# Norm chains at stage borders by half blocks, in a twelve-stage network on one core

## The chip, the core and the metric

One core of a Trainium2 chip runs the whole program. The metric is the device time of one execution in microseconds (us). TensorE (PE) multiplies matrices, VectorE (DVE) and ScalarE (ACT) do the elementwise work, GpSimd (POOL) a little of it, and SyncE (SP) issues the loads. The engines run their own instruction streams in order and wait for each other through semaphores.

## The reference

A sequence of 256 tokens with 1024 features goes through two small models, one behind the other. Every sub-layer reads a normed copy of the residual `h` and adds its product to `h`:

```python
# first model: layer 0 = gated linear recurrence (HGRN), layer 1 = sparse attention (DSA)
hn = rms_norm(h, attn_norm[layer]);  h = h + mixer(hn)
h  = h + conv_ffn(rms_norm(h, ffn_norm[layer]), ...)      # SwiGLU, width 2816, conv of 3 taps
h  = rms_norm(h, final_norm)
# second model: layer 0 = hybrid of attention and conv, layer 1 = gated linear attention (GLA)
h  = h + 0.5 * rms_norm(swiglu(rms_norm(h, g[0]), ffn1), g[1])
h  = h + rms_norm(mixer(rms_norm(h, g[2])), g[3])
h  = h + 0.5 * rms_norm(swiglu(rms_norm(h, g[4]), ffn2), g[5])

def rms_norm(x, gain):                                    # over the 1024 features
    return x * rsqrt(mean(x * x) + 1e-6) * gain
```

So there are six feed-forward stages, ffn 0 to ffn 5, and four mixers, in the order HGRN, ffn 0, DSA, ffn 1, (final norm), ffn 2, hybrid, ffn 3, ffn 4, GLA, ffn 5. Between any two stages stands a chain: product, (norm and gain of the product), add to `h`, norm of `h`, transpose, next product.

## The kernel before, in words

**Products in three parts.** Each float32 operand is split into a high part (fp32r, made by ACT, line 547 for weights and 603 for activations) and a low part (made by DVE, lines 1049, 1108 and 1001, or POOL, line 469). `three` (lines 1561 to 1563) issues high by high, high by low and low by high. The weights come as 1 MB slabs into a ring of four slots (`raw0` to `raw3`).

**Tokens in two blocks.** The 256 tokens are two blocks of 128 (`tb` 0 and 1). A stage's product lies in PSUM as two banks of 512 columns for each block, banks `2*tb` and `2*tb+1`. In an ffn the down projection adds into these banks slab by slab; the last two slabs (`a` and `b_`) run block by block, so that block 0 is complete (`half_done`) while PE still works on block 1.

**The chain of a block at a border**, in the order of the streams, for a stage whose product is normed (after ffn 2 to 5 and after the last two mixers):

- ACT `square_product`: squares of the 1024 columns in PSUM with their sum (L578), then the root (L580);
- DVE `gain_block`: product times gain, two instructions of 512 columns (L1030), after the squares, since both read the banks; reciprocal (L993); `add_normed_block`: one instruction of 1024 columns into `h` (L1035). Without such a norm there is only `add_block` (L1022), 1024 columns;
- ACT `square_h`: squares and sum of `h` (L578), root (L580); DVE reciprocal and `scaled_block` (L1012), two of 512 columns, which gives `xn`;
- PE `turn_block`: 8 transposes of `xn` (L1647); ACT 8 high parts `x_hi` with the gain (L603); DVE 8 low parts `x_lo` (L1001); then the next product, which waits for `x_lo` chunk by chunk (L1561).

PE has other work to put between the blocks. In ffn 0, 1, 3 and 5 block 1 is turned in the middle of the second slab of block 0; in ffn 2 and ffn 4 (`late`) after it; in each case the product of block 1 then needs its `x_lo`. After the 24 matmuls of block 1's first slab PE transposes the first products of block 0 (`turn_tokens`, L1705); these must have been copied out of PSUM by ACT (L614) first. In front of ffn 2, ffn 4, the hybrid and GLA, PE runs 8 bf16 matmuls on zeros (`keep_warm`, L1639) before block 0 is turned.

**What else stands in the streams there.** ACT loads another function table with `preload` (L572): Sqrt at the end of an ffn, Silu at its start. ACT makes the high part of the next slab, `high_one` (L547); DVE makes the low parts of the next stage's first two slabs, `c_` and `d`, at the end of an ffn (`low_one`, L1049), before it looks at the product.

Of the kernel before, what the change touches and what calls it, by code (L numbers as in the profile page):

```python
# [18 lines left out]
F32 = mybir.dt.float32  # L19
# [113 lines left out]
def build(nc, A, out):  # L133
    with ExitStack() as ctx:
# [26 lines left out]
        ssq = small[:, 0:2]  # L161
        std = small[:, 4:6]
        rstd = small[:, 6:8]
        eps_col, eps_col4 = small[:, 152:153], small[:, 153:154]
# [73 lines left out]
        h_ready, y_gained = sem("h_ready"), sem("y_gained")  # L238
        rms_sq = sem("rms_sq")
# [5 lines left out]
        half_done = sem("half_done")  # L245
# [218 lines left out]
        def _(pool):  # L464
# [26 lines left out]
            pool.memset(eps_col4, 4.0 * EPS).then_inc(eps_set, 1)  # L491
# [44 lines left out]
        def _(act):  # L536
# [37 lines left out]
            def square(tb, src, half=False):  # L574

                one = slice(tb, tb + 1)
                scale = (2.0 if half else 1.0) * D ** -0.5
                act.activation(squares, src, ACT.Square, scale=scale, accum_out=ssq[:, one]).then_inc(rms_sq, 1)  # L578
                act.wait_ge(rms_sq, want(rms_sq))
                act.activation(std[:, one], ssq[:, one], ACT.Sqrt, bias=eps_col4 if half else eps_col).then_inc(rms_std, 1)  # L580

            def square_h(tb, updates):

                if updates:
                    act.wait_ge(h_ready, 2 * updates - 1 + tb)
                else:
                    act.wait_ge(x_in[tb], 16)
                square(tb, h[:, tb, :])

            def square_product(tb, last, half):  # L590
# [107 lines left out]
            act.wait_ge(eps_set, 2)  # L698
            preload(ACT.Sqrt)
            for tb in range(NTB):  # L700
                square_h(tb, 0)
# [59 lines left out]
            def normed_ffn(f, norm, updates, conv=False, f_conv=0, after_out=True, last=None, half=False, gain=None):  # L761
# [22 lines left out]
            want(half_done, 4)  # L784
            square_h(0, 2)
# [52 lines left out]
            def square_when(tb, times):  # L838
                act.wait_ge(h_ready, times)
                square(tb, h[:, tb, :])  # L840

# [111 lines left out]
        def _(dve):  # L953
# [34 lines left out]

            def inverse_rms(tb):
                one = slice(tb, tb + 1)  # L990
                want(rms_sq)
# [15 lines left out]
            def scaled_block(tb):  # L1007

                r = inverse_rms(tb)
# [27 lines left out]
            def final_block(tb):  # L1037
                r = inverse_rms(tb)
                dve.scalar_tensor_tensor(h[:, tb, :], h[:, tb, :], r, gain_row, ALU.mult, ALU.mult).then_inc(h_ready, 1)
# [5 lines left out]
            def low_one(slot):  # L1045
# [4 lines left out]
                    .then_inc(slab_ready[slot], 1)  # L1050

# [1053 lines left out]
```

## Time and profile before

| | |
|---|---|
| median of 3 runs | 1763.93 us (1763.34 to 1767.48) |
| the profiled execution | 1765.37 us, span 1763.3 us |
| PE busy | 1676.9 us (95%) |
| DVE, ACT, POOL busy | 1065.5 (60%), 847.4 (48%), 176.2 us (10%) |
| mean granted clock of PE | 0.978 of full |

PE is busy 95% of the span, and the slices in which it isn't are the start, the attention parts of the mixers and the stage borders. The view of waits gives, for each pair of a waiting and a releasing line, how long PE stood still; the timeline of an engine gives each instruction's start, duration and, in brackets, the idle time before it with what ended it. A number in tenths or as a share under the clock is the granted clock against 2.4 GHz: 0.5 is 1.2 GHz.

### The profile page before, as it was taken

What the parts mean: (1) busy time and instruction counts of PE and PEld (TensorE: products, weight loads), DVE (VectorE), ACT (ScalarE), POOL (GpSimd) and SP (SyncE); (2) the same over time, 40 slices, a digit from 0 to 9 for tenths busy, and PEclk for the clock granted to TensorE, in tenths of its full rate; (3) what the DMA queues carried; (4) which work ended last, traced back from release to release, by engine and by line L of the source; (5) the groups of instructions that cost most, each with busy time, mean ns of one, the idle gap of its engine ahead of it and who ended that gap; (6) DMA issues with size and microseconds to landing.
All of it is one profiled execution on the core that took longest, in us unless ns stands there. A gap on an engine that the chain in (4) does not pass through costs nothing. (4 is left out here: it accounts for less than half of the span.)

```text
span 1763.3 us, 28914 instructions
## 1 busy us (share of the span) xinstructions
PE 1676.9 (95%) x11809; PEld 1562.4 (89%) x11818; DVE 1065.5 (60%) x1484; ACT 847.4 (48%) x1137; POOL 176.2 (10%) x48
## 2 busy tenths in 40 slices
PE   7999999999999998999988589999999999899998
PEld 6998999989799997999987479999899989889997
DVE  1796776747567766544539955545644475765444
ACT  6323655543665546444454364444544465354443
POOL 5351000021600000000057200000000000000000
PEclk9999999989999999999999699999999999999999
DMA  8623477643236563655642315556355644425552
GB/s 268 201 72 97 159 196 215 192 142 122 92 121 204 169 218 122 197 189 174 214 150 96 96 36 193 189 190 215 132 191 188 204 151 163 143 86 190 189 180 83
DMA packets 220068, 283.49 MB, mean 161 GB/s; under 512 B 13004, under 2 KB 197315, under 8 KB 219987
## 3 DMA queue, kind: packets, MB, share of 16 engines
q1 hardware_dynamic: 218499, 278.18, 48.7%
q10 hardware_dynamic: 1488, 4.17, 0.7%
q8 instruction: 59, 0.97, 0.2%
q14 instruction: 22, 0.18, 0.0%
HBM read 280.88 MB, written 1.44 MB: 160 GB/s over the span
## 5 line engine op out<-in xcount | busy, mean ns | idle before, releaser
L1561 PE MATMUL ps<-x_hi,w_hi 128*128 128x256 f32 (+1 forms) x2368 | 672.8, 284 | 1.1 <-POOL w_lo L469 0.8
L1562 PE MATMUL ps<-x_lo,w_hi 128*128 128x256 f32 (+1 forms) x2368 | 671.6, 284 | 0.0
L1563 PE MATMUL ps<-x_hi,w_lo 128*128 128x256 f32 (+1 forms) x2368 | 671.5, 284 | 0.0
L547 ACT ACTIVATE w_hi<-raw 128x2048 fp32r<-128x2048 f32 x262 | 498.8, 1911 | 219.3 <-PE ps L1563 199.8
L1108 DVE TENSOR_TENSOR w_lo<-raw,w_hi 128x2048 fp32r<-128x2048 f32 x162 | 371.3, 2292 | 260.3 <-ACT w_hi L547 260.3
L1561 PEld LDWEIGHTS ps<-x_hi,w_hi 128*128 128x128 f32 (+1 forms) x2368 | 455.4, 192 | 5.9 <-issue 2.7
L1562 PEld LDWEIGHTS ps<-x_lo,w_hi 128*128 128x128 f32 (+1 forms) x2368 | 455.3, 192 | 2.3
L1563 PEld LDWEIGHTS ps<-x_hi,w_lo 128*128 128x128 f32 (+1 forms) x2368 | 455.1, 192 | 0.2
L1561 PE MATMUL ps<-w_hi,x_hi 128*128 128x256 f32 (+3 forms) x688 | 222.0, 323 | 16.3 <-DVE x_lo L1001 13.4
L469 POOL TENSOR_TENSOR w_lo<-raw,w_hi 128x2048 fp32r<-128x2048 f32 x32 | 160.1, 5026 | 759.0 <-ACT w_hi L547 759.0
L1562 PE MATMUL ps<-w_lo,x_hi 128*128 128x256 f32 (+3 forms) x688 | 216.7, 315 | 0.0
L1563 PE MATMUL ps<-w_hi,x_lo 128*128 128x256 f32 (+3 forms) x688 | 216.5, 315 | 0.0
L1561 PE MATMUL ps<-w_hi,g_hi 128*128 128x512 f32 x480 | 187.5, 391 | 0.0
L1562 PE MATMUL ps<-w_lo,g_hi 128*128 128x512 f32 x480 | 187.5, 391 | 0.0
L1563 PE MATMUL ps<-w_hi,g_lo 128*128 128x512 f32 x480 | 186.7, 389 | 0.0
L1049 DVE TENSOR_TENSOR w_lo<-raw,w_hi 128x2048 fp32r<-128x2048 f32 x68 | 154.1, 2287 | 29.5 <-ACT w_hi L547 29.5
L1561 PEld LDWEIGHTS ps<-w_hi,x_hi 128*128 128x128 f32 x688 | 134.7, 196 | 27.9 <-issue 9.3
L1563 PEld LDWEIGHTS ps<-w_hi,x_lo 128*128 128x128 f32 x688 | 135.0, 196 | 7.3
L1562 PEld LDWEIGHTS ps<-w_lo,x_hi 128*128 128x128 f32 x688 | 135.0, 196 | 6.8
L653 ACT ACTIVATE g_hi<-arena 128x256 fp32r<-128x256 f32 x120 | 44.0, 410 | 154.7 <-PE ps L1563 148.7
L1563 PEld LDWEIGHTS ps<-w_hi,g_lo 128*128 128x128 f32 x480 | 90.1, 188 | 19.2
L1561 PEld LDWEIGHTS ps<-w_hi,g_hi 128*128 128x128 f32 x480 | 90.3, 188 | 17.1
(172 smaller groups left out, 1373.3 us busy)
## 6 DMA issues: line engine op xcount, KB each, us to landing
raw<-in_ffn_w_in SPq DMA_DIRECT2D x88, 1024.0 KB, 5.1
raw<-in_ffn_w_up SPq DMA_DIRECT2D x44, 1024.0 KB, 5.1
raw<-in_ffn_w_out SPq DMA_DIRECT2D x44, 1024.0 KB, 4.9
raw<-in_ffn_w_down SPq DMA_DIRECT2D x22, 1024.0 KB, 5.0
raw<-in_hgrn_w_in SPq DMA_DIRECT2D x16, 1024.0 KB, 5.9
raw<-in_gla_w_in SPq DMA_DIRECT2D x12, 1024.0 KB, 5.5
raw<-in_hyb_w_in SPq DMA_DIRECT2D x10, 1024.0 KB, 5.2
raw<-in_dsa_w_in SPq DMA_DIRECT2D x6, 1024.0 KB, 5.4
```

What stands on the lines that cost most here:

```text
L469: pool.tensor_tensor(w_lo[slot][:, :], raw[slot][:, :], w_hi[slot][:, :].bitcast(F32), ALU.subtract)\
L547: act.activation(w_hi[slot][:, :], raw[slot][:, :], ACT.Copy).then_inc(hi_done[slot], 1)
L653: act.activation(dst[:, b, :], ff_g[:, b, :], ACT.Copy).then_inc(gt_hi[b], 1)
L1049: dve.tensor_tensor(w_lo[slot][:, :], raw[slot][:, :], w_hi[slot][:, :].bitcast(F32), ALU.subtract)\
L1108: dve.tensor_tensor(w_lo[slot][:, :], raw[slot][:, :], w_hi[slot][:, :].bitcast(F32), ALU.subtract)\
L1561: pe.matmul(out_ap, a_hi, b_hi, start=start, stop=False, skip_group_check=True)
L1562: pe.matmul(out_ap, a_hi, b_lo, start=False, stop=False, skip_group_check=True)
L1563: return pe.matmul(out_ap, a_lo, b_hi, start=False, stop=stop, skip_group_check=True)
```

## The change

- **Half blocks.** The norm chain works by 512 columns: two squares with a sum each, the add into `h` in two instructions, with the new semaphores `h_half` (first half of `h` written) and `y_half` (first bank of the product complete). The root needs the sum of the two sums and epsilon: DVE adds epsilon to the first sum (`add_eps`, 1 column), and ACT takes that as the bias of the root. The root waits for this (`rms_eps`).
- **Bank by bank.** In an ffn's last two slabs PE finishes the first bank of a block before its second; the number of matmuls stays. `y_half` is given 6 matmuls before the block's end (3 in the mixers' output products, whose order stays).
- **Moved.** ACT makes the high part of `c_` before the squares of block 1 of `h`, and loads the Silu table after the 8 high parts of block 1; at ffn 2 only the high parts of block 1 go ahead of table load and high part of the slab. DVE makes the second half of `d`'s low part (1024 of 2048 columns) after block 0 has been added into `h`.

```diff
-ssq = small[:, 0:2]
+ssq = small[:, 0:4]
+ssq_eps = small[:, 112:114]
...
-    def square(tb, src, half=False):
-
-        one = slice(tb, tb + 1)
+    def square_half(tb, part, src, scale):
+
+        at = 2 * tb + part
+        act.activation(squares[:, part * 512:part * 512 + 512], src, ACT.Square, scale=scale, accum_out=ssq[:, at:at + 1])\
+            .then_inc(rms_sq, 1)
+
+    def root_of_sum(tb):
+
+        act.wait_ge(rms_sq, want(rms_sq, 2))
+        act.wait_ge(rms_eps, want(rms_eps))
+        act.activation(std[:, tb:tb + 1], ssq[:, 2 * tb + 1:2 * tb + 2], ACT.Sqrt, bias=ssq_eps[:, tb:tb + 1])\
+            .then_inc(rms_std, 1)
+    def square_when(tb, times):
+
+        act.wait_ge(h_half, times)
+        square_half(tb, 0, h[:, tb, 0:512], D ** -0.5)
+        act.wait_ge(h_ready, times)
+        square_half(tb, 1, h[:, tb, 512:D], D ** -0.5)
+        root_of_sum(tb)
...
+    def square_first(tb):
+
+        act.wait_ge(x_in[tb], 16)
+        for part in range(2):
+            square_half(tb, part, h[:, tb, part * 512:part * 512 + 512], D ** -0.5)
+        root_of_sum(tb)
...
+        act.wait_ge(y_half, want(y_half))
+        square_half(tb, 0, ps[:, 2 * tb, :], scale)
         if tb == 0:
             act.wait_ge(half_done, want(half_done))
         else:
             act.wait_ge(slab_used[last], ring.uses[last] + 1)
-        square(tb, ps[:, 2 * tb:2 * tb + 2, :].rearrange("p b n -> p (b n)"), half)
+        square_half(tb, 1, ps[:, 2 * tb + 1, :], scale)
+        root_of_sum(tb)
...
     def columns(a, z, times):
@@ -771,10 +791,10 @@
         split_normed(0, *norm)
         if after_out and last is not None:
             square_product(1, last, half)
+        high_one(c_)
         square_h(1, updates)
+        split_normed(1, *norm)
         preload(ACT.Silu)
-        high_one(c_)
-        split_normed(1, *norm)
...
+    split_normed(1, "norm_g_2", 0)
     preload(ACT.Silu)
     high_one(FFN_SLOTS[2][2])
-    split_normed(1, "norm_g_2", 0)
...
+    def add_eps(tb, eps):
+
+        dve.wait_ge(rms_sq, want(rms_sq, 2) - 1)
+        dve.tensor_scalar(ssq_eps[:, tb:tb + 1], ssq[:, 2 * tb:2 * tb + 1], eps, None, ALU.add).then_inc(rms_eps, 1)
+
...
 
+        add_eps(tb, EPS)
...
     def add_block(tb, last):
-        product_done(tb, last)
-        dve.tensor_tensor(h[:, tb, :], h[:, tb, :], flat(2 * tb, 2), ALU.add).then_inc(h_ready, 1)
-
-    def gain_block(tb, last):
-
-        product_done(tb, last)
-        dve.wait_ge(rms_sq, want(rms_sq, 0) + 1)
-        for half in range(2):
+        for half, done in enumerate((h_half, h_ready)):
+            at = slice(half * 512, half * 512 + 512)
+            if half == 0:
+                dve.wait_ge(y_half, want(y_half))
+            else:
+                product_done(tb, last)
+            dve.tensor_tensor(h[:, tb, at], h[:, tb, at], flat(2 * tb + half), ALU.add).then_inc(done, 1)
+
+    def gain_block(tb, last, eps):
...
+        def gain(half):
             at = slice(half * 512, half * 512 + 512)
             dve.tensor_tensor(xn[:, tb, at], flat(2 * tb + half), gain_row[:, at], ALU.mult).then_inc(y_gained, 1)
+
+        add_eps(tb, eps)
+        gain(0)
+        product_done(tb, last)
+        dve.wait_ge(rms_sq, want(rms_sq, 0))
+        gain(1)
...
-        dve.scalar_tensor_tensor(h[:, tb, :], xn[:, tb, :], r, h[:, tb, :], ALU.mult, ALU.add).then_inc(h_ready, 1)
+        for half, done in enumerate((h_half, h_ready)):
+            at = slice(half * 512, half * 512 + 512)
+            dve.scalar_tensor_tensor(h[:, tb, at], xn[:, tb, at], r, h[:, tb, at], ALU.mult, ALU.add).then_inc(done, 1)
...
+        for half, done in enumerate((h_half, h_ready)):
+            at = slice(half * 512, half * 512 + 512)
+            dve.scalar_tensor_tensor(h[:, tb, at], h[:, tb, at], r, gain_row[:, at], ALU.mult, ALU.mult).then_inc(done, 1)
...
+    def low_part(slot, part):
+
+        at = slice(part * 1024, part * 1024 + 1024)
+        if part == 0:
+            u, _ = lows.take(slot)
+            dve.wait_ge(hi_done[slot], u + 1)
+        ins = dve.tensor_tensor(w_lo[slot][:, at], raw[slot][:, at], w_hi[slot][:, at].bitcast(F32), ALU.subtract)
+        if part == 1:
+            ins.then_inc(slab_ready[slot], 1)
...
             dve.wait_ge(gain_in, want(gain_in, 16))
-            gain_block(0, last)
+            gain_block(0, last, 4.0 * EPS)
             add_normed_block(0)
+            low_part(FFN_SLOTS[f][3], 1)
             scaled_block(0)
-            gain_block(1, last)
+            gain_block(1, last, 4.0 * EPS)
             split_normed(0, *norm)
             add_normed_block(1)
         scaled_block(1)
...
             low_one(c_)
-            low_one(d)
+            low_part(d, 0)
...
                 for half in range(2):
                     ins = three(ps[:, 2 * tb + half, :], acts(k, tb * P, P), weights(s, kk * D + half * 512, 512),
                                 k == 0, k == NK - 1)
+                    if k == NK - 1 and half == 0:
+                        ins.then_inc(y_half, 1)
...
         for tb in range(NTB):
-            for b in range(2):
-                ins = down_block(a, tb, b, False)
+            for half in range(2):
+                for b in range(2):
+                    ins = down_part(a, tb, b, half, False)
             if tb == NTB - 1:
                 ins.then_inc(slab_used[a], 1)
             for b in range(2):
                 pe.wait_ge(g_ready, 2 * q0 + 2 * (NF - 1) + b + 1)
-                if tb == NTB - 1 and b == 1:
-                    before_end()
-                ins = down_block(b_, tb, b, True)
+                ins = down_part(b_, tb, b, 0, True)
+            ins.then_inc(y_half, 1)
+            if tb == NTB - 1:
+                before_end()
+            for b in range(2):
+                ins = down_part(b_, tb, b, 1, True)
             ins.then_inc(half_done if tb == 0 else slab_used[b_], 1)
```

The streams at the places that change, instruction by instruction. ACT at the entry of ffn 4: squares and root of the product of block 0 stand three rows above; `w_hi<-raw` is the high part of slab `c_`, `x_hi` the high parts of a block, `arena<-ps 128x512` the copy that `turn_tokens` waits for. Before:

```order
L603 ACTIVATE x_hi<-ps,cols 128x128 x8
L578 ACTIVATE arena,small<-h 128x1024
L580 ACTIVATE small<-small 128x1
L572 ACT_TABLE_LOAD
L572 ACTIVATE small<-small 128x1
L547 ACTIVATE w_hi<-raw 128x2048
L603 ACTIVATE x_hi<-ps,cols 128x128 x8
L759 DMA arena<-in_norm_g 128x1024
L614 ACTIVATE arena<-ps 128x512
```

Now, at the same place:

```order
L623 ACTIVATE x_hi<-ps,cols 128x128 x8
L547 ACTIVATE w_hi<-raw 128x2048
L577 ACTIVATE arena,small<-h 128x512 x2
L584 ACTIVATE small<-small 128x1
L623 ACTIVATE x_hi<-ps,cols 128x128 x8
L572 ACT_TABLE_LOAD
L572 ACTIVATE small<-small 128x1
L779 DMA arena<-in_norm_g 128x1024
L634 ACTIVATE arena<-ps 128x512
```

The second block's high parts no longer stand behind the table load and the slab's high part; the copy stands directly behind the table load. ACT at the entry of ffn 2, now:

```order
L577 ACTIVATE arena,small<-h 128x512 x2
L584 ACTIVATE small<-small 128x1
L623 ACTIVATE x_hi<-ps,cols 128x128 x8
L572 ACT_TABLE_LOAD
L572 ACTIVATE small<-small 128x1
L547 ACTIVATE w_hi<-raw 128x2048
L779 DMA arena<-in_norm_g 128x1024
L634 ACTIVATE arena<-ps 128x512
```

Here the slab's high part stands between the block's high parts and the copy; before, the row `x_hi ... x8` stood behind `w_hi<-raw`, directly ahead of the copy. DVE at the end of ffn 1, from the last low parts of the activations (`x_lo`) on; `w_lo<-raw` are low parts of slabs, `h<-h,ps` is the add. Before:

```order
L1140 TENSOR_TENSOR x_lo<-arena,x_hi 128x256 x2
L1049 TENSOR_TENSOR w_lo<-raw,w_hi 128x2048 x2
L1022 TENSOR_TENSOR h<-h,ps 128x1024
L993 RECIPROCAL small<-small 128x1
L1039 SCALAR_TENSOR_TENSOR h<-h,small,arena 128x1024
```

Now, from the same instruction on:

```order
L1190 TENSOR_TENSOR x_lo<-arena,x_hi 128x256 x2
L1087 TENSOR_TENSOR w_lo<-raw,w_hi 128x2048
L1096 TENSOR_TENSOR w_lo<-raw,w_hi 128x1024
L1049 TENSOR_TENSOR h<-h,ps 128x512 x2
L1096 TENSOR_TENSOR w_lo<-raw,w_hi 128x1024
L1009 TENSOR_SCALAR small<-small 128x1
L1014 RECIPROCAL small<-small 128x1
L1077 SCALAR_TENSOR_TENSOR h<-h,small,arena 128x512 x2
```

Half of a slab's low part has moved behind the add, and ahead of the small add of epsilon for which ACT's root waits.

## Rows read from the trace of the kernel before

**Rows 1.** Waits of PE: who it waited for, us in total, times, longest.

```profile
PE ps L1561 <- DVE x_lo L1001: 13.7, 16, 2.2
PE ps L1647 <- DVE xn L1012: 10.8, 5, 4.2
...
PE ps L1647 <- DVE x_lo L1001: 5.5, 1, 5.5
```

**Rows 2.** Timeline of PE, entry of ffn 5: start, us, line, tiles, [idle before, releaser].

```profile
1564.15 0.35 PE L1561 MATMUL ps<-w_hi,x_hi 128*128 128x256 f32 x1 [0.45 <-DVE x_lo L1001]
...
1570.68 1.09 PE L1647 MATMUL ps<-const,xn 128*128 128x128 f32 x8 [1.99 <-DVE xn L1012]
...
1574.17 0.38 PE L1561 MATMUL ps<-w_hi,x_hi 128*128 128x256 f32 x1 [0.97 <-DVE x_lo L1001]
```

**Rows 3.** Timeline of ACT, entry of ffn 5.

```profile
1551.96 1.03 ACT L578 ACTIVATE arena<-ps 128x1024 f32<-128x1024 f32 x1 [3.92 <-PE ps L1563]
...
1557.11 0.29 ACT L580 ACTIVATE small<-small 128x1 f32<-128x1 f32 x1
```

**Rows 4.** Timeline of DVE, entry of ffn 5.

```profile
1553.21 1.29 DVE L1030 TENSOR_TENSOR xn<-ps,arena 128x512 f32<-128x512 f32 x2 [4.53 <-ACT arena L578]
...
1554.61 1.28 DVE L1035 SCALAR_TENSOR_TENSOR h<-xn,small,h 128x1024 f32<-128x1024 f32 x1
```

**Rows 5.** Timeline of PE, entry of ffn 3.

```profile
1051.06 1.09 PE L1647 MATMUL ps<-const,xn 128*128 128x128 f32 x8 [1.98 <-DVE xn L1012]
```

**Rows 6.** Timeline of ACT, entry of ffn 3.

```profile
1033.16 1.28 ACT L580 ACT_TABLE_LOAD   x1
```

**Rows 7.** Timeline of PE, entry of ffn 4.

```profile
1236.75 1.67 PE L1639 MATMUL ps<-const 128*128 128x512 bf16 x7
...
1245.66 1.04 PE L1647 MATMUL ps<-const,xn 128*128 128x128 f32 x8
...
1251.64 0.60 PE L1705 MATMUL ps<-const,arena 128*128 128x128 f32 x4
```

**Rows 8.** Timeline of PE, entry of the gated linear attention.

```profile
1439.78 1.04 PE L1647 MATMUL ps<-const,xn 128*128 128x128 f32 x8
...
1441.26 0.39 PE L1561 MATMUL ps<-w_hi,x_hi 128*128 128x256 f32 x1 [0.45 <-DVE x_lo L1001]
```

**Rows 9.** Timeline of ACT, entry of the gated linear attention.

```profile
1440.20 1.14 ACT L603 ACTIVATE x_hi<-ps,cols 128x128 fp32r<-128x128 f32 x4 [1.68 <-PE ps L1647]
```

**Rows 10.** Timeline of PE, entry of ffn 2.

```profile
692.95 1.09 PE L1647 MATMUL ps<-const,xn 128*128 128x128 f32 x8 [1.24 <-DVE xn L1012]
...
702.14 1.03 PE L1647 MATMUL ps<-const,xn 128*128 128x128 f32 x8
...
704.26 0.39 PE L1561 MATMUL ps<-w_hi,x_hi 128*128 128x256 f32 x1 [1.08 <-DVE x_lo L1001]
...
707.23 0.60 PE L1705 MATMUL ps<-const,arena 128*128 128x128 f32 x4
```

**Rows 11.** Timeline of ACT, entry of ffn 2.

```profile
700.01 1.28 ACT L572 ACT_TABLE_LOAD   x1
...
701.41 1.90 ACT L547 ACTIVATE w_hi<-raw 128x2048 fp32r<-128x2048 f32 x1
...
705.21 0.64 ACT L614 ACTIVATE arena<-ps 128x512 f32<-128x512 f32 x1
```

**Rows 12.** Timeline of DVE, end of ffn 0.

```profile
362.56 4.49 DVE L1049 TENSOR_TENSOR w_lo<-raw,w_hi 128x2048 fp32r<-128x2048 f32 x2
```

**Rows 13.** Timeline of PE, entry of the sparse attention.

```profile
370.56 1.06 PE L1647 MATMUL ps<-const,xn 128*128 128x128 f32 x8 [1.29 <-DVE xn L1012]
```

**Rows 14.** Timeline of PE, entry of the hybrid mixer.

```profile
894.97 1.94 PE L1647 MATMUL ps<-const,xn 128*128 128x128 f32 x8 [4.24 <-DVE xn L1012]
```

**Rows 15.** Timeline of PE, entry of ffn 0.

```profile
186.74 0.39 PE L1561 MATMUL ps<-w_hi,x_hi 128*128 128x256 f32 x1 [0.42 <-DVE x_lo L1001]
```

**Rows 16.** Busy us (and instructions) of each engine in a stretch, PE's clock, DMA share.

```profile
694.80:697.00 2.20, 2.17 (x11) 2.20 (x12) 1.69 (x8) 2.13 (x7) 0.00 (x0) 0.56 0.00 0
```

More of the change, by code:

```diff
@@ L237, in build @@
         gain_in, gate_in = sem("gain_in"), sem("gate_in")
-        h_ready, y_gained = sem("h_ready"), sem("y_gained")
-        rms_sq = sem("rms_sq")
+        h_half, h_ready, y_gained = sem("h_half"), sem("h_ready"), sem("y_gained")
+        rms_sq, rms_eps = sem("rms_sq"), sem("rms_eps")
         eps_set, rms_std = sem("eps_set"), sem("rms_std")
@@ L244, in build @@
         up_half = sem("up_half")
-        half_done = sem("half_done")
+        half_done, y_half = sem("half_done"), sem("y_half")
         conv_in = [sem(f"conv_in{b}") for b in range(2)]
@@ L490, in _ @@
             pool.memset(eps_col, EPS).then_inc(eps_set, 1)
-            pool.memset(eps_col4, 4.0 * EPS).then_inc(eps_set, 1)
             pool.memset(zeros, 0.0).then_inc(zeros_set, 1)
@@ L572, in preload, with square_h, square_product @@
                 act.activation(small[:, 154:155], eps_col, func)
-            def square(tb, src, half=False):
-                one = slice(tb, tb + 1)
-                scale = (2.0 if half else 1.0) * D ** -0.5
[L578 to L590, printed above, removed]
+            def square_half(tb, part, src, scale):
[13 more added lines that the diff above has]
+                root_of_sum(tb)
+            def square_h(tb, updates):
+                square_when(tb, 2 * updates - 1 + tb)
+            def square_first(tb):
[3 more added lines that the diff above has]
+                root_of_sum(tb)
+            def square_product(tb, last, half):
+                scale = (2.0 if half else 1.0) * D ** -0.5
+                act.wait_ge(y_half, want(y_half))
+                square_half(tb, 0, ps[:, 2 * tb, :], scale)
                 if tb == 0:
@@ L697, in _ @@
             act.dma_start(rows[p0:p0 + k, t, :], src).then_inc(first_in, 16)
-            act.wait_ge(eps_set, 2)
+            act.wait_ge(eps_set, 1)
             preload(ACT.Sqrt)
             for tb in range(NTB):
-                square_h(tb, 0)
+                square_first(tb)
             preload(ACT.Sigmoid)
@@ L784, in _ @@
             want(half_done, 4)
+            want(y_half, 4 * NTB)
             square_h(0, 2)
@@ L1020, in add_block @@
             def add_block(tb, last):
-                product_done(tb, last)
-                dve.tensor_tensor(h[:, tb, :], h[:, tb, :], flat(2 * tb, 2), ALU.add).then_inc(h_ready, 1)
-            def gain_block(tb, last):
-                product_done(tb, last)
-                dve.wait_ge(rms_sq, want(rms_sq, 0) + 1)
-                for half in range(2):
+                for half, done in enumerate((h_half, h_ready)):
[6 more added lines that the diff above has]
+            def gain_block(tb, last, eps):
+                want(y_half)
+                def gain(half):
                     at = slice(half * 512, half * 512 + 512)
                     dve.tensor_tensor(xn[:, tb, at], flat(2 * tb + half), gain_row[:, at], ALU.mult).then_inc(y_gained, 1)
+                add_eps(tb, eps)
[3 more added lines that the diff above has]
+                gain(1)
             def add_normed_block(tb):
@@ L1064, in add @@
                     else:
-                        gain_block(tb, last)
+                        gain_block(tb, last, EPS)
                         add_normed_block(tb)
@@ L1421, in _ @@
             add_block(0, last)
+            low_part(FFN_SLOTS[1][3], 1)
             dve.wait_ge(gain_in, want(gain_in, 16))
@@ L1549, in _ @@
                     for tb in range(NTB):
-                        gain_block(tb, FFN_SLOTS[5][1])
+                        gain_block(tb, FFN_SLOTS[5][1], 4.0 * EPS)
                         add_normed_block(tb)
@@ L1721, in up, with down_part @@
                     features(d, 5 + 2 * odd, P, P, SEQ).then_inc(slab_used[d], 1)
-                def down_block(s, tb, b, last, first=False):
-                    for half in range(2):
-                        hi, lo = (x_hi, x_lo) if last else (g_hi, g_lo)
-                        g = (hi[:, b, tb * P:tb * P + P], lo[:, b, tb * P:tb * P + P])
-                        ins = three(ps[:, 2 * tb + half, :], g, weights(s, b * D + half * 512, 512), first and b == 0,
-                                    last and b == 1)
-                    return ins
+                def down_part(s, tb, b, half, last, first=False):
+                    hi, lo = (x_hi, x_lo) if last else (g_hi, g_lo)
+                    g = (hi[:, b, tb * P:tb * P + P], lo[:, b, tb * P:tb * P + P])
+                    return three(ps[:, 2 * tb + half, :], g, weights(s, b * D + half * 512, 512), first and b == 0,
+                                 last and b == 1)
                 def down(i, first=False):
@@ L1735, in down @@
                         for b in range(2):
-                            ins = down_block(a, tb, b, False, first)
+                            for half in range(2):
+                                ins = down_part(a, tb, b, half, False, first)
                     ins.then_inc(slab_used[a], 1)
@@ L1761, in ffn @@
                 for tb in range(NTB):
-                    for b in range(2):
-                        ins = down_block(a, tb, b, False)
+                    for half in range(2):
+                        for b in range(2):
+                            ins = down_part(a, tb, b, half, False)
                     if tb == NTB - 1:
```

9 lines of the change are left out of this document (3 added, 6 removed).

## Prediction

> **What bounds the kernel now.** I read the view of waits first, for PE alone: PE is busy for 95% of the span, so an edit on ACT or DVE counts only where PE stands still for it. At the borders it stands still for two things: 16 waits for `x_lo` (13.7 us) and 5 waits of the transposes for `xn` (10.8 us), beside 5.5 us once at the start, where the transposes of block 1 wait for `x_lo` [rows 1]. That is 30 us, and with the tail behind the last matmul it is all that this change can reach. Next I read PE's timeline at each of the borders, to see which of the waits a shorter norm chain ends, and then ACT's and DVE's there, to see what the chain is made of. The reader is to see that the borders are of three kinds: those where PE reaches the transposes before `xn` is there (hybrid 4.24, ffn 5 1.99, ffn 3 1.98, DSA 1.29, ffn 2 1.24 [rows 2, 5, 10, 13, 14]); those where it waits for `x_lo` because ACT did a table load and a slab's high part first (ffn 0, ffn 2 to 5); and those where PE's own work or its 8 warming matmuls cover the chain (block 0 at ffn 4, both blocks at GLA).
>
> **What a shorter chain is worth, by one block.** At ffn 5 the squares of the product start at 1551.96 and the product is gained from 1553.21, when the squares of all 1024 columns and their sum are done; `h` is written from 1554.61 [rows 3, 4]. That is 2.65 us. An ACT instruction of 512 columns from PSUM takes 0.64 and one of 1024 1.03 [rows 3, 11]; the 1024-column square with its sum takes 1.15 to the next step (1.25 until the gain starts), so I take 0.73 for one of 512. The first square lies beside PE's last matmuls, and the first gain beside the second square. What is left behind the product is 0.8 (second square, slightly late because `y_half` comes only 3 matmuls ahead in the mixers), 0.6 (second gain: two take 1.29) and 0.2 (reciprocal): 1.6. **Saved: 1.05 to 1.1.** From the start of the write to `h` to the root it is 1557.11 - 1554.61 = 2.50. In halves: first write 0.75 and hand-over, first square 0.73, second square 0.73: 2.27. **Saved: 0.23.** Without the norm of the product the 1.22 us add becomes 0.66 behind the product, and the first half's square is done by then: about 1.0 saved in all, if DVE is free. The added epsilon (one column, some 0.16 like a reciprocal) waits for the first sum and is over before the second; where it stands first in DVE's stream it costs 0.1. Splitting costs in total some 0.07 for each pair on DVE and 0.25 for each pair on ACT, on engines that are free for much of the time.
>
> Here the Trainium skill speaks against the change: "VectorE: DVE Perf Modes", on the SBUF-source errata, says that each instruction of ScalarE or VectorE pays a fixed latency and that tiles of at least 512 elements should be used. The rows agree with a fixed part (0.64 against 1.03 for half the columns), and 512 is just what the change keeps; the price is in the 0.25 above.
>
> **Border by border.**
>
> *Start, -0.5.* Nothing is split on PE here; ACT's stream of squares, table load, slab high part and `x_hi` leads directly to the 5.5 us wait [rows 1]. Two blocks with 0.25 more each stand ahead of it, and the second root waits for the epsilon that DVE adds behind both halves of block 0's `xn`. Nothing hides it: 0.5 later.
>
> *ffn 0 and ffn 1, +0.42 each.* `xn` is no longer waited for here. Only the 0.42 us wait for block 1's `x_lo` [rows 15] (0.43 in ffn 1) goes, since `x_hi` now comes before table load and slab. ACT's copy for `turn_tokens` moves to the time after the table load, but PE has 12 and 24 matmuls ahead of that.
>
> *DSA, +1.0.* DVE, not the product, was late here: the two slab low parts run from 362.56 for 4.49 us, to 367.05, and the add follows without a wait [rows 12]. Half of the second (1.1) moves behind the add. The root then waits for it and for the epsilon, so that the root comes 1.0 earlier; PE's wait of 1.29 [rows 13] shrinks by that.
>
> *ffn 2, +1.15 and -1.2.* Block 0: the same 1.1 at the add, two `h` steps with 0.23 each less what the epsilon costs: `xn` 1.15 earlier, nearly the whole wait of 1.24 [rows 10], until the warming matmuls bound it. Block 1: `x_hi` can start 0.42 after the transposes start and the product follows 1.48 after them, as GLA shows, which has no table load there [rows 8, 9]. The 24 matmuls to `turn_tokens` take 707.23 - 704.26 = 2.97 [rows 10]: PE is there 4.45 after the transposes, against 5.09 before. But the copy now stands behind the high parts (2.0: from 705.21 - 701.41 less 1.8), the table load (1.40) and the slab's high part (1.8), and takes 0.64 [rows 11]: 0.42 + 2.0 + 1.4 + 1.8 + 0.64 = 6.3. **A new wait of 1.8 us on the copy takes the place of the one of 1.08, and `turn_tokens` starts 1.2 later than before.**
>
> *Hybrid, +0.4.* Block 0 is covered by 1.67 us of warming matmuls. Block 1's chain starts behind the split of block 0, so only the two late steps (0.2 and 0.23) count of the 4.24 [rows 14].
>
> *ffn 3, +1.75, and ffn 5, +2.35.* At ffn 5 block 0's chain ends 1.3 earlier; ACT's two slab high parts follow it, DVE's low parts follow these, then block 0's `x_lo` (PE's 0.45 goes [rows 2]), then block 1's gain. With 0.23 of its own and 0.1 lost, the transposes of block 1 come 1.4 earlier (of the wait of 1.99, 0.45 is just PE's own earlier arrival). Then 0.97 goes as in ffn 0 [rows 2]. At ffn 3 a table load of 1.28 stands between squares and root [rows 6] and takes the gain's share: 0.65 at block 0, 0.8 at the transposes [rows 5], and the same 0.97.
>
> *ffn 4, +1.5.* Block 0 sits behind warming matmuls at 1236.75 and gains nothing. `turn_tokens` started 1251.64 - 1245.66 = 5.98 after the transposes [rows 7]; now PE could at 4.45, and the copy is done at 0.42 + 2.0 + 1.4 + 0.64, 4.5. The slab's high part, 1.9 us, fits into ACT's gap before block 1's `h` is there.
>
> *GLA, 0.* Covered. *End, +1.0.* 1.1 at the product, with the last write in two halves 0.1 longer; the store is unchanged.
>
> Sum: -0.5 + 0.42 + 0.42 + 1.0 - 0.05 + 0.4 + 1.75 + 2.35 + 1.5 + 1.0 = 8.3. The profiled execution took 1765.37 (span 1763.3 and 2.1 around it), so it would take 1757.1; the median of the runs shown is 1.4 lower: **1755.6 us**. Inside the mixers, PE waits for chains that start from the projections and move with them; I cost them at nothing. The rows of last slabs now put six matmuls in a row on one bank; other products of this kernel put 24 on one, at the same pace.
>
> **The rivals.**
>
> *A. The chain gives less than the halves promise.* ACT is in order, and the slab's high part now stands ahead of block 1's squares at ffn 3 and ffn 5. My sum has it end within 0.1 us of the time when they could start. For: at ffn 5 the margin is 0.05. Against: its slot has been released for some us. If it comes a full 1.9 late at both, 3.8 goes; if each hand-over costs 0.1 more, 1 to 2: 1759.5. Chance 0.2.
>
> *B. PE's clock gains too.* At ffn 2 the granted clock fell to 0.5 for a time behind the idle entry (0.56 over 694.8 to 697 [rows 16]), there are 11 matmuls in 2.2 us where 2.97 hold 24; by an estimate from these the fall cost 1.5. With the wait of 1.24 gone ffn 2's entry looks like ffn 4's, where PE goes from the warming matmuls straight to the transposes: 1.5 more, 1754.1. If DSA's entry, too, were spared half clock, 1 to 3 more. Chance 0.25, and it gives the low end.
>
> *C. Slower.* The new wait of 1.8 us at ffn 2 and the shifted rest meet the clock instead: PE falls to 1.2 GHz at entries where it held. One costs 1.5 (as at ffn 2 now). It decides from six more on: 9 lost against 8.3. At all ten it is 15 lost, 1770.6. For: idle time ahead of a fall at the hybrid and ffn 2. Against: ffn 3 and ffn 5 have 1.98 and 1.99 idle and their transposes take 1.09, not the 1.94 of the hybrid's [rows 2, 5, 14], and the change shortens every other gap. Chance 0.04.
>
> *D. The moved parts do nothing* because what PE waits for is set elsewhere, and only the end and the `x_lo` waits change: about 4 gained, 1760. Chance 0.06, within A's end of the range.
>
> *E. The table load holds ACT for longer where work stands right behind it.* The rows show 1.28 for the load and the next slab 1.40 after its start [rows 11], with nothing between. If another 1.4, as much as the whole step, came ahead of the copy at ffn 2 and ffn 4, 2.8 would go: 1758.4. Chance 0.02. The Trainium skill, "ScalarE: Activation LUTs", on what a table load costs, has such a part: 1.38 us of drain behind a load of 1.28, for every switch of sets; the trace shows no such gap.
>
> **How the numbers follow.** Forecast as summed, 1753 to 1758.5: chance 0.43. With A, B and D, 8 in 10 lie between **1751.5 and 1760.5**. About 0.3% (5.3 us) is what a measurement of this kernel can tell from no change, so faster means under 1758.6: the forecast and B whole, part of A and D: 0.77. Same 0.19; slower 0.04, which is C.
>
> **What would show it.** In the profile after: no wait of over 0.5 us for `x_lo` at ffn 3, 4, 5; waits for `xn` of 0.3 at DSA, about 1 at ffn 5, 1.9 at ffn 3, 3.9 at the hybrid, none at ffn 2; a new wait of `turn_tokens` for ACT's copy of about 1.8 at ffn 2 and at most 0.3 at ffn 4; the first projection 0.5 later; a squares-to-write distance at ffn 5 of 1.6 in place of 2.65. I am wrong if the wait for `xn` at ffn 3 and ffn 5 doesn't move the transposes earlier by 0.8 and 1.4, if `turn_tokens` waits elsewhere, or if the granted clock changes at an entry by more than one fall.

## The result, and the profile after

| | before | changed |
|---|---|---|
| median of 5 runs each, us | 1763.93 (1763.34 to 1769.85) | 1755.48 (1754.40 to 1756.64) |
| ratio to before | | 0.9937 [0.9922, 0.9952] |
| the profiled execution, us | 1765.37 | 1754.8 |
| its span, us | 1763.3 | 1752.9 |

Faster by 8.45 us; 1755.6 had been forecast. The page's first lines of the changed kernel:

```profile
span 1752.9 us, 29090 instructions
## 1 busy us (share of the span) xinstructions
PE 1676.3 (96%) x11818; PEld 1561.8 (89%) x11818; DVE 1072.6 (61%) x1545; ACT 854.8 (49%) x1205; POOL 176.0 (10%) x47
```

PE's busy time is what it was (1676.9). DVE and ACT got 7.1 and 7.4 us more, the price of the halves. What went is idle time of PE, as the view of its waits says (columns: who waits for whom, us in total, times, longest):

```profile
PE ps L1612 <- DVE x_lo L1022: 7.7, 10, 2.2
PE ps L1698 <- DVE xn L1034: 7.1, 4, 3.9
...
PE ps L1698 <- DVE x_lo L1022: 5.8, 1, 5.8
...
PE ps L1758 <- ACT arena L634: 1.8, 1, 1.8
```

Against [rows 1] the product's waits for `x_lo` fell from 13.7 to 7.7 and the transposes' waits for `xn` from 10.8 to 7.1. There is one new line, 1.8 us for ACT's copy. (L1612 is L1561 of before, L1698 is L1647, L1758 is L1705, L1690 is L1639.) A list of waits doesn't say what each place gained in time, so I laid both PE timelines side by side and took, from one fixed event to the next (first product of a stage, transposes of block 0, of block 1, `turn_tokens`), by how much the stretch had become shorter:

| stretch | forecast | shorter by |
|---|---|---|
| start, to the first product | -0.5 | -0.42 |
| ffn 0, ffn 1: transposes of block 1 to `turn_tokens` | 0.42 each | 0.67 each |
| DSA: to the transposes of block 0 | 1.0 | 1.03 |
| ffn 2: to the transposes of block 0 | 1.15 | 1.30 |
| ffn 2: block 1's transposes to `turn_tokens` | -1.2 | -1.36 |
| hybrid: to the transposes of block 1 | 0.4 | 0.30 |
| ffn 3: to block 1's transposes; from there to `turn_tokens` | 0.8 and 0.97 | 0.95 and 1.22 |
| ffn 4: block 1's transposes to `turn_tokens` | 1.5 | 1.34 |
| ffn 5: as ffn 3 | 1.4 and 0.97 | 1.58 and 1.23 |
| end, behind the last matmul | 1.0 | 0.89 |
| **sum** | **8.3** | **9.4** |

The spans differ by 10.4. Of the other 1.0, 0.35 is the input, which landed earlier in the execution after, so that ACT's first square came earlier; that isn't counted as a gain. The rest is in stretches whose work the change leaves alone: +1.59 in HGRN's output product, +1.42 in ffn 2's block 0, +0.68 in the hybrid, -1.44 and -1.48 in and behind GLA, and small ones. In all of these five the granted clock is at 1.2 GHz over different times in the two executions. (In the hybrid it is so for longer at the entry in before, and for longer in the middle in the changed kernel.) ffn 2's fall is the one of [rows 16]. A wider stretch round it, and one in HGRN, read like this in before (columns: stretch and its length, busy us and instructions of PE, PE's loads, DVE, ACT and POOL, then the granted clock, the DMA share and GB/s):

```profile
692.00:696.00 4.00, 2.27 (x14) 2.06 (x15) 3.76 (x11) 2.75 (x10) 0.00 (x0) 0.88 0.00 0
...
155.00:160.00 5.00, 5.00 (x16) 3.97 (x15) 2.35 (x9) 0.00 (x0) 0.00 (x0) 0.66 0.24 77
```

and in the changed kernel:

```profile
692.00:696.00 4.00, 4.00 (x36) 4.00 (x36) 2.79 (x7) 1.71 (x6) 0.00 (x0) 1.00 0.00 0
...
155.00:160.00 5.00, 5.00 (x24) 4.06 (x23) 2.43 (x9) 0.00 (x0) 0.00 (x0) 1.00 0.30 96
```

At 155 the change is far away: from the first product to the transposes at 150.7 it is 132.74 us before and 132.76 in the changed kernel, and a wait of 1.84 us for `x_lo` at 154.3 stands in both. Yet 16 matmuls ran in this stretch in one execution and 24 in the other.

The places one by one. PE's timeline of the changed kernel (start, us, line, tiles, [idle before, releaser]) at the entries of DSA, ffn 2, hybrid, ffn 3, ffn 4 and ffn 5:

```profile
367.35 0.33 PE L1698 MATMUL ps<-const,xn 128*128 128x128 f32 x1 [0.32 <-DVE xn L1034]
...
685.92 1.90 PE L1690 MATMUL ps<-const 128*128 128x512 bf16 x8
687.78 1.09 PE L1698 MATMUL ps<-const,xn 128*128 128x128 f32 x8
...
695.55 1.04 PE L1698 MATMUL ps<-const,xn 128*128 128x128 f32 x8
...
889.48 0.30 PE L1698 MATMUL ps<-const,xn 128*128 128x128 f32 x1 [3.94 <-DVE xn L1034]
...
1043.93 0.77 PE L1698 MATMUL ps<-const,xn 128*128 128x128 f32 x5 [1.74 <-DVE xn L1034]
...
1237.29 1.04 PE L1698 MATMUL ps<-const,xn 128*128 128x128 f32 x8
...
1241.93 0.66 PE L1758 MATMUL ps<-const,arena 128*128 128x128 f32 x4
...
1562.39 1.09 PE L1698 MATMUL ps<-const,xn 128*128 128x128 f32 x8 [1.08 <-DVE xn L1034]
...
1564.74 0.28 PE L1612 MATMUL ps<-w_hi,x_hi 128*128 128x256 f32 x1
...
1567.62 0.60 PE L1758 MATMUL ps<-const,arena 128*128 128x128 f32 x4
```

They answer to [rows 13, 10, 14, 5, 7, 2]: 1.29 became 0.32; 1.24 is gone, and the warming matmuls run straight into the transposes; 4.24 became 3.94, 1.98 became 1.74, 1.99 became 1.08; `turn_tokens` at ffn 4 stands 4.64 behind the transposes, not 5.98. At ffn 5 twelve matmuls of block 0 follow the transposes, before as now; the thirteenth is the first that needs block 1's `x_lo`. Before it waited 0.97 (at 1574.17 in [rows 2]), now it starts at 1564.74 without a wait, and `turn_tokens` stands 5.23 behind the transposes, not 6.46. The shorter norm chain, ACT at ffn 5's block 0:

```profile
1544.58 0.60 ACT L577 ACTIVATE arena<-ps 128x512 f32<-128x512 f32 x1 [3.29 <-PE ps L1614]
1545.07 0.20 ACT L577 ACTIVATION_READ_ACCUMULATOR arena<-ps 128x1 f32 x1
1545.26 0.60 ACT L577 ACTIVATE arena<-ps 128x512 f32<-128x512 f32 x1
...
1549.05 0.29 ACT L584 ACTIVATE small<-small 128x1 f32<-128x1 f32 x1
```

and DVE beside it:

```profile
1545.37 0.15 DVE L1009 TENSOR_SCALAR small<-small 128x1 f32<-128x1 f32 x1 [3.43 <-ACT arena L577]
1545.44 1.30 DVE L1057 TENSOR_TENSOR xn<-ps,arena 128x512 f32<-128x512 f32 x2
...
1546.85 1.41 DVE L1070 SCALAR_TENSOR_TENSOR h<-xn,small,h 128x512 f32<-128x512 f32 x2
```

From the square of the second bank to the write of `h` it is 1546.85 - 1545.26 = 1.59. Before it was 2.65 from the one square of the whole block [rows 3, 4]. From that write to the root it is 2.20, not 2.50. The pitch of two squares is 0.68; I had 0.73.

### The profile page after: what moved, and what is told of

Same layout as the page of the kernel before. It is cut to its first block and busy times, and to the rows that moved or that the text cites. A ratio compares the mean times of both kernels' runs of the same rounds, so it can differ in the third digit from the quotient of the medians.

```text
span 1752.9 us, 29090 instructions
## 1 busy us (share of the span) xinstructions
PE 1676.3 (96%) x11818; PEld 1561.8 (89%) x11818; DVE 1072.6 (61%) x1545; ACT 854.8 (49%) x1205; POOL 176.0 (10%) x47
## 3 DMA queue, kind: packets, MB, share of 16 engines
HBM read 280.88 MB, written 1.44 MB: 161 GB/s over the span
## 5 line engine op out<-in xcount | busy, mean ns | idle before, releaser
L1612 PE MATMUL ps<-x_hi,w_hi 128*128 128x256 f32 (+1 forms) x2368 | 672.6, 284 | 1.1 <-POOL w_lo L470 0.7
L1158 DVE TENSOR_TENSOR w_lo<-raw,w_hi 128x2048 fp32r<-128x2048 f32 x162 | 371.2, 2291 | 260.3 <-ACT w_hi L547 260.3
L1612 PEld LDWEIGHTS ps<-x_hi,w_hi 128*128 128x128 f32 (+1 forms) x2368 | 455.0, 192 | 5.9 <-issue 2.7
L1612 PE MATMUL ps<-w_hi,x_hi 128*128 128x256 f32 (+3 forms) x688 | 220.9, 321 | 10.2 <-DVE x_lo L1022 7.3
L1612 PE MATMUL ps<-w_hi,g_hi 128*128 128x512 f32 x480 | 187.5, 391 | 0.0
L1087 DVE TENSOR_TENSOR w_lo<-raw,w_hi 128x2048 fp32r<-128x2048 f32 x63 | 143.6, 2287 | 36.0 <-ACT w_hi L547 36.0
L1612 PEld LDWEIGHTS ps<-w_hi,x_hi 128*128 128x128 f32 x688 | 134.1, 195 | 20.5 <-issue 7.8
L1612 PEld LDWEIGHTS ps<-w_hi,g_hi 128*128 128x128 f32 x480 | 90.4, 188 | 17.1
```

The costliest lines, as they stand in the source:

```text
L1087: dve.tensor_tensor(w_lo[slot][:, :], raw[slot][:, :], w_hi[slot][:, :].bitcast(F32), ALU.subtract)\
L1158: dve.tensor_tensor(w_lo[slot][:, :], raw[slot][:, :], w_hi[slot][:, :].bitcast(F32), ALU.subtract)\
L1612: pe.matmul(out_ap, a_hi, b_hi, start=start, stop=False, skip_group_check=True)
```

## The experiments

Each is compared with runs of the kernel before that were made beside it; the ratios have their 95% intervals. Beside the first four experiments the kernel before had a median of 1764.87 (11 runs), beside the last four 1764.04 (17 runs). Lengths of stretches come from one profiled execution of each kernel, the medians from 5 to 12.

### ACT's order alone undone

```diff
-high_one(c_)
 square_h(1, updates)
-split_normed(1, *norm)
 preload(ACT.Silu)
+high_one(c_)
+split_normed(1, *norm)
...
 # ffn 2
-split_normed(1, "norm_g_2", 0)
 preload(ACT.Silu)
 high_one(FFN_SLOTS[2][2])
+split_normed(1, "norm_g_2", 0)
```

> The changed kernel with ScalarE's order as before: table load and slab high part ahead of block 1's high parts. Theory (the gain is a sum of waits at single borders): against the changed kernel ffn 0 and ffn 1 lose 0.7 each, ffn 3, ffn 4 and ffn 5 1.2 to 1.3 each at turn_tokens, ffn 2 gains 1.4 (no wait on the copy); the waits for x_lo of 0.4 to 2.0 us are back; in all 3.7 slower than 1755.5, so 1759.2. Rival (halves and clock gave everything, the moves nothing): 1755.5, and the leads at turn_tokens as in the changed kernel.

Measured: 1757.37 us, ratio 0.9955 [0.9938, 0.9972]: 1.9 slower than the changed kernel where 3.7 had been forecast. The stretches behind block 1's transposes gave 0.41 and 0.42 at ffn 0 and ffn 1 (with the moves 0.67), 0.00 at ffn 3 (1.22), 0.30 at ffn 4 (1.34) and -0.01 at ffn 5 (1.23). So the moves are worth 0.26 + 0.25 + 1.22 + 1.04 + 1.24 = 4.0 there; at ffn 0 and ffn 1 the earlier chain alone would have brought more than half. ffn 2 is the place to read closely. PE with ACT's old order:

```profile
697.78 1.04 PE L1698 MATMUL ps<-const,xn 128*128 128x128 f32 x8
701.23 0.58 PE L1612 MATMUL ps<-w_hi,x_hi 128*128 128x256 f32 x1 [2.40 <-DVE x_lo L1022]
...
705.51 0.60 PE L1758 MATMUL ps<-const,arena 128*128 128x128 f32 x4
```

ACT:

```profile
696.98 1.28 ACT L572 ACT_TABLE_LOAD   x1
...
698.38 1.89 ACT L547 ACTIVATE w_hi<-raw 128x2048 fp32r<-128x2048 f32 x1
...
700.18 2.16 ACT L623 ACTIVATE x_hi<-ps,cols 128x128 fp32r<-128x128 f32 x8
```

The wait for `x_lo` is 2.40, not the 1.08 of before [rows 10]: block 1's transposes come earlier (1.44 by the clock that held in block 0's product), table load and slab part do not. From the transposes to `turn_tokens` it is 7.73, of which 1.31 is a low clock (24 matmuls took 4.28, not 2.97); without it 6.42, against 6.45 in the changed kernel. **At ffn 2 neither order is better by these two profiles**, apart from what the clock does: one waits in front of the product, the other behind it. The halves were never run alone. What is left of the gain with the old order is 5.4 by stretches (ffn 2 taken without its low clock), 1.2 of it from the moved low part, as the next experiment shows.

### The low part in one piece

```diff
-low_part(d, 0)
+low_one(d)
...
-low_part(FFN_SLOTS[f][3], 1)    # three places
```

> The changed kernel, with VectorE's low part of slab d made in one instruction of 2048 columns ahead of the product again. Theory: only DSA and ffn 2 pay, where VectorE is behind the product, 1.0 and 1.1: 1757.6; at the hybrid, ffn 4 and GLA the chain of block 0 ends 0.5 later, which the warming matmuls cover. Rival (the half is hidden anyway, the halves of the add gave the gain at DSA): under 0.4 in all, 1755.8.

Measured: 1755.49 us, ratio 0.9949 [0.9933, 0.9964]. The forecast of 1757.6 missed: the median is no different from the changed kernel's, as the rival had it. By stretches DSA's entry gained 0.45 and not 1.03, ffn 2's 0.71 and not 1.30, 1.2 in all; the other places that the change touches gave the same. The median doesn't show this 1.2. DVE at ffn 2's entry shows why it isn't the whole 1.1:

```profile
678.81 4.49 DVE L1087 TENSOR_TENSOR w_lo<-raw,w_hi 128x2048 fp32r<-128x2048 f32 x2
683.21 1.28 DVE L1049 TENSOR_TENSOR h<-h,ps 128x512 f32<-128x512 f32 x2
```

Even with the add as late as before, squares in halves end earlier. And in the changed kernel the root at ffn 2 waits for the epsilon, which DVE adds behind the low part's second half:

```profile
683.97 0.30 ACT L584 ACTIVATE small<-small 128x1 f32<-128x1 f32 x1 [0.52 <-DVE small L1009]
```

So at DSA the 1.0 was right and its parts were not: 0.58 for the moved low half, 0.45 for the halves of add and squares.

### The last slabs in their old order

```diff
-for half in range(2):
-    for b in range(2):
+for b in range(2):
+    for half in range(2):
...
-                        ins = down_part(b_, tb, b, 0, True)
-                    ins.then_inc(y_half, 1)
...
-                    for b in range(2):
-                        ins = down_part(b_, tb, b, 1, True)
...
+                        for half in range(2):
+                            ins = down_part(b_, tb, b, half, True)
+                            if b == 1 and half == 0:
+                                ins.then_inc(y_half, 1)
```

> The changed kernel, with the last two slabs of an ffn in the order of before; the first bank is complete 3 matmuls ahead of the end of a block and not 6. Theory: nothing at the borders (VectorE is behind at DSA and ffn 2, warming matmuls cover the others) and at most 0.2 at the very end: 1755.6. Rival (the halves pay only because the first bank is ready 1.4 us early): 0.5 at each of five exits, 1758.

Measured: 1754.53 us, ratio 0.9942 [0.9925, 0.9959]. That is 1.0 under the changed kernel, where the same had been forecast, and the ranges of the two overlap. Of the places in the table only DSA's entry changed, 0.93 for 1.03. `y_half` three matmuls before the end is early enough, and the product at one bank costs nothing that can be seen. This part of the change does nearly nothing.

### The slab's high part early at ffn 2 as well

```diff
+high_one(FFN_SLOTS[2][2])
 split_normed(0, "norm_g_2", 0)
...
 preload(ACT.Silu)
-high_one(FFN_SLOTS[2][2])
```

> The changed kernel, with ScalarE's high part of slab c_ at ffn 2 ahead of block 0's high parts, in the gap of 1.25 us before them, so that the copy stands directly behind the table load. Theory: block 0's x_lo comes 0.55 later, the wait of 1.83 on the copy goes, turn_tokens starts 1.3 to 1.4 earlier: 1754.1. Rival (the copy is held by something else, or the slab's part isn't ready that early): 1755.5 or slower.

Measured: 1751.77 us, ratio 0.9924 [0.9907, 0.9940]; 1754.1 had been forecast. ACT:

```profile
688.71 1.90 ACT L547 ACTIVATE w_hi<-raw 128x2048 fp32r<-128x2048 f32 x1
...
700.38 1.28 ACT L572 ACT_TABLE_LOAD   x1
...
701.78 0.58 ACT L634 ACTIVATE arena<-ps 128x512 f32<-128x512 f32 x1
```

PE:

```profile
697.72 1.09 PE L1698 MATMUL ps<-const,xn 128*128 128x128 f32 x8
...
702.42 0.66 PE L1758 MATMUL ps<-const,arena 128*128 128x128 f32 x4
```

`turn_tokens` stands 4.70 behind the transposes, not 6.45, and the new wait is gone; block 1's transposes come 0.37 later, since block 0's chain gets its high parts later. Net 1.38, as forecast (1.3 to 1.4). That is the price of the new wait by stretches, and the changed kernel need not pay it. The median fell by 3.7; the rest is taken up under "Open" below. In the changed kernel the same piece of ACT reads:

```profile
698.16 1.28 ACT L572 ACT_TABLE_LOAD   x1
...
699.57 1.90 ACT L547 ACTIVATE w_hi<-raw 128x2048 fp32r<-128x2048 f32 x1
701.37 0.58 ACT L634 ACTIVATE arena<-ps 128x512 f32<-128x512 f32 x1
```

and PE, with the wait that had been forecast as 1.8:

```profile
702.00 0.66 PE L1758 MATMUL ps<-const,arena 128*128 128x128 f32 x4 [1.83 <-ACT arena L634]
```

### The kernel before with nothing but ACT's moves

```diff
+high_one(c_)
 square_h(1, updates)
+split_normed(1, *norm)
 preload(ACT.Silu)
-high_one(c_)
-split_normed(1, *norm)
...
 # ffn 2
+split_normed(1, "norm_g_2", 0)
 preload(ACT.Silu)
 high_one(FFN_SLOTS[2][2])
-split_normed(1, "norm_g_2", 0)
```

> The kernel before with ScalarE's moved order alone (slab high part ahead of block 1's squares, table load behind block 1's high parts; ffn 2 as in the change). Theory: the waits for x_lo of block 1 go and nothing else: ffn 0, ffn 1 0.7 each, ffn 3, ffn 4, ffn 5 1.2 to 1.3 each, ffn 2 1.2 slower as long as its clock falls as before: 3.9 faster than before at equal clock falls, 1760. The first run of this study has the mirror image, the change without these moves, where ffn 0 lost only 0.3, since there the shorter chain had already moved the table load. Rival (moves and halves need each other): under 2 faster.

Measured: 1762.54 us (12 runs), ratio 0.9985 [0.9976, 0.9995]: 1.5 us gained, a miss by 2.5. The stretches that the moves touch gave 0.67, 0.68, 1.33 and 1.22 as in the changed kernel (ffn 0, 1, 4, 5), -1.42 at ffn 2 and -0.26 at ffn 3, where a low clock ate 1.48:

```profile
1050.00:1053.50 3.50, 2.97 (x20) 2.98 (x21) 2.71 (x10) 2.48 (x9) 0.00 (x0) 0.77 0.19 51
```

Another 2.0 went in DSA, most of it where the low clock that every one of these kernels has there lasted longer. One thing bears on rival B: ffn 2's entry is as long here as before (0.01 shorter), and the low clock in block 0's product is absent all the same: the clock is 1.00, and the stretch is 1.37 shorter. So the fall of before doesn't follow from the long entry alone.

```profile
692.00:696.00 4.00, 2.01 (x15) 1.54 (x14) 3.23 (x9) 2.72 (x12) 0.00 (x0) 1.00 0.00 0
```

### Fewer warming matmuls

The kernel with the early slab part, and in place of 8 warming matmuls at each of four entries 0, and then 3:

```diff
-WARM_NORMED = 8
+WARM_NORMED = 0
```

> The change with the slab's part of ffn 2 early, and no warming matmuls ahead of the transposes of block 0 (ffn 2, hybrid twice, ffn 4, GLA). Theory: since the halves xn is there before TensorE has ended the product, so at ffn 4 and GLA the 8 warming matmuls are now the longest thing ahead of the transposes: 1.6 less each, at the hybrid 0.8 (block 1's chain starts earlier), at ffn 2 nothing: 4.0 less than 1751.8, 1747.8, if the clock holds. Rival (the clock needs them): one fall more at each of the four entries, 1.4 to 1.5 each: 1753.5.

```diff
-WARM_NORMED = 8
+WARM_NORMED = 3
```

> As the one with no warming matmuls, with 3 in place of 8. Theory: 3 take 0.7 where 8 take 1.9, 1.1 less at ffn 4 and GLA and 0.5 at the hybrid: 1749.1. Rival (clock): as before with one fall more at some of them, 1751 to 1753.

Measured: 1748.67 us with none, ratio 0.9907 [0.9890, 0.9924]; 1749.07 with three, ratio 0.9905 [0.9889, 0.9920]. The stretch to an entry is that from `turn_tokens` of the stage ahead to the transposes of block 0. With none, the stretches to the entries of hybrid, ffn 4 and GLA are 1.56, 1.62 and 1.57 shorter than before's, but those up to block 1's transposes longer than with eight, by 0.75, 0.58 and 0.57; with three they are 1.04, 1.08 and 1.03 shorter and give back 0.22, 0.03 and 0.04. ffn 2's entry is as with eight in both (1.30), since `xn` bounds it. In ffn 2's block 0 the clock fell with none:

```profile
692.00:696.00 4.00, 3.94 (x18) 3.97 (x19) 3.18 (x11) 2.95 (x11) 0.00 (x0) 0.50 0.00 0
```

and block 0's stretch took 10.53 us against 8.14 with eight. It stayed up with three:

```profile
692.00:696.00 4.00, 3.91 (x33) 3.71 (x32) 2.56 (x7) 2.02 (x7) 0.00 (x0) 1.00 0.00 0
```

The two can't be told apart by their medians (1747.8 and 1749.1 had been forecast), and their profiles aren't typical: that with none is of the slowest of its six runs (1753.13; four of the others took 1747.6 to 1748.7), that with three of the fastest (1747.26, span 1745.3). Whether the clock falls at ffn 2 without warming in most executions isn't shown. Both beat both kernels; the version with three is 15.0 us under the median of before and 6.4 under the changed kernel's.

### The changed kernel a second time

Nothing edited; run to see how far the same program's clock and time vary.

> The changed kernel once more, on the same chip as the last three. Both theories: 1755.5 within 1.5; its stage lengths agree with the first profile within 0.1 us wherever the clock doesn't fall, and the falls stand elsewhere or are one more or fewer.

Measured: 1755.65 us, ratio 0.9943 [0.9927, 0.9958]. Behind the start each stretch of the table above agrees with the first profile within 0.03 us. The clock doesn't repeat: behind GLA nothing was lost this time (+0.03 for -1.48), but 1.58 between ffn 2's `turn_tokens` and the hybrid, where the first profile lost 0.04. The clock is low right behind the new wait:

```profile
702.15 1.01 PE L1758 MATMUL ps<-const,arena 128*128 128x128 f32 x4 [1.84 <-ACT arena L634]
```

```profile
700.00:704.00 4.00, 2.16 (x12) 1.96 (x11) 2.36 (x2) 3.90 (x3) 0.00 (x0) 0.79 0.00 1
704.00:708.00 4.00, 4.00 (x30) 4.00 (x28) 2.22 (x1) 0.76 (x2) 0.00 (x0) 0.79 0.68 219
```

Of five profiles with this wait of 1.83 or 1.84 (the changed kernel twice, low part whole, slabs in old order, moves alone) two have it there, this one and the old slab order (1.56 lost). Of the three with the slab part early, which haven't the wait, none has. The kernel with ACT's old order has a wait of 2.40 there instead, and a fall behind it.

## Why the prediction was right

The time came out within 0.2 us of the forecast, and that much agreement is luck: by stretches the change gives 9.4 and not 8.3, and the low clocks elsewhere, which give and take as much again, are not in the sum. The mechanism held: the named waits went, at the named places, and the named new wait came.

- **Terms that held.** Start, DSA, ffn 2, hybrid, ffn 4 and end each within 0.2. The new wait of `turn_tokens` at ffn 2 is there, 1.83 for 1.8, and the copy at ffn 4 is not waited for. That the squares-to-write distance would be 1.6 was right to 0.01. The fixed part of an instruction was read from 0.64 against 1.03, which both read PSUM; the squares of `h` in SBUF show it too, 0.64 for 512 columns against 1.06 for 1024.
- **The term that was mis-sized: the waits for `x_lo` that go.** I took them at the idle time listed (0.42, 0.43, 0.97, 0.97), and they were worth 0.67, 0.67, 1.22 and 1.23. Before, at ffn 0, the last matmul ahead of the wait starts at 186.04 and is drawn 0.28 long, and the next starts at 186.74 with 0.42 idle [rows 15]; but matmuls of this shape follow each other every 0.12. The wait costs 0.70 - 0.12 = 0.58, and the first matmul behind it another 0.11, its successor starting 0.23 later, not 0.12 (before, ffn 0):

```profile
185.92 0.28 PE L1562 MATMUL ps<-w_lo,x_hi 128*128 128x256 f32 x1
186.04 0.28 PE L1563 MATMUL ps<-w_hi,x_lo 128*128 128x256 f32 x1
...
186.97 0.28 PE L1562 MATMUL ps<-w_lo,x_hi 128*128 128x256 f32 x1
```

Over the four places that is 1.0 of the 1.1 that was missing. ffn 3 gave 2.17 for 1.75 and ffn 5 2.81 for 2.35 by this and 0.2 more from the chain.
- **The price of the order at ffn 2 was right as a number, wrong as a cause.** I charged 1.2 to the moved copy, on top of a kernel whose clock had fallen. The experiment with the old order shows 6.42 (with its own low clock taken off) from transposes to `turn_tokens` against 6.45: the 5.09 of before goes with a low clock that had made PE late at the transposes, when ACT's table load was already over. Once the clock holds, ACT's row of high parts, table load, slab part and copy is the bound in either order; the +1.42 of the clock, which the forecast kept for rival B, and the -1.36 cancel. Only the early slab part takes it away (1.38).
- **DSA and ffn 2, block 0.** The sums were right; half of what I gave to the moved low half belongs to the halves of add and squares.
- **Rivals.** *A* did not occur: at ffn 3 and ffn 5 the slab part ended in time, 0.95 and 1.58. *B* named a low clock that is indeed gone, from all seven profiles with the shorter entry and warming matmuls. That its reason was the right one isn't shown: with an entry as long as before one of two profiles had no fall either. And the gain there was taken by the copy. *C* occurred at one place and small: the clock is low behind ffn 2's new wait in two of five profiles, 1.6 each; five more such places would have been needed. *D* is right for one part only, the order by banks (0.1 in all). *E*: the copy at ffn 4 starts 1.40 after the table load does; nothing longer. The Trainium skill ("ScalarE: Activation LUTs", "What ACT_TABLE_LOAD costs") has a drain behind the load; no profile here shows one.
- **Open.** By stretches ACT's moves are worth 4.0 us in the changed kernel and 3.7 alone (0.67 + 0.68 + 1.22 + 1.33 + 1.22 - 1.42, ffn 3's without its low clock). In the medians they show as 1.9 and 1.5. A low clock behind the new wait, in two of five profiles, would explain some 0.6 of the difference (the one behind the wait of the old order works the other way). One more place stands out in the ten profiles: from GLA's transposes of block 1 to the next transposes it is 96.8 us before, with ACT's moves alone and with ACT's old order, but 97.9 to 98.3 in the changed kernel (twice), with the low part whole and with the slabs in old order. With the early slab part it is 97.0 and 97.1, and 97.7 without warming. So the 1.44 lost in GLA was not lost in one profile only: 1.1 to 1.4 went there in all four. That is some 1.2 of the 2.1 missing for the moves in the changed kernel, and together with the 0.6 it brings the early slab part, 1.38 by stretches, to about 3 of the 3.7 of its median. For the moves alone it explains nothing. Why more is lost there in these kernels, and whether it is the change's doing, isn't shown.

## What to carry to other kernels

Cut a norm chain where two engines take turns on one tile: while one squares the second half the other gains the first, and of 2.65 us 1.6 are left. Behind such a cut look at what stood in the streams to cover the old chain, here 8 warming matmuls and a slab part: they have become the bound. Taking the slab part and five of the eight matmuls out of the way was worth another 6.4 us in the median. Before charging a wait to an edit, check that the time of before wasn't held up by something else, here a clock that fell.

## What the hardware showed that I had not expected

- **A listed wait understates itself by a quarter of a microsecond** in rows of 128x256 products: removing 0.42 gave 0.67, removing 0.97 gave 1.22, within 0.02 in every profile with ACT's moves (at ffn 3 of the moves alone once its low clock, 1.48, is taken off).
- **The granted clock differs between executions of one program at one place.** At 155 us it fell in six of the ten profiles and not in the other four, the changed kernel's two among these; in all but one of the ten (the one without warming) the stretch from the first product to the transposes at 150.7 is as long to 0.04 us. One such fall cost 1.3 to 1.6 us, as much as a whole border gains by this change.
- **The accumulator is an instruction of its own.** Each square with a sum is followed by a read of 0.18 to 0.20 us, overlapping by 0.1, so two halves cost 0.68 each where one whole took 1.15 (1551.96 to the root at 1553.11 before, entry of ffn 5).
